# Up-projection of the latents in a two-block decoder kernel: query columns regrouped into rotary, turned and plain tiles, each emptied by one engine; values projected ahead of keys

## The reference, cut to what matters

```python
q = (_rmsnorm(q_lat, g_q_lat[i]) @ w_q_up[i]).reshape(bsz, s, N_HEADS, QK_DIM)      # 384 -> 8 x 96
kv = (_rmsnorm(kv_lat, g_kv_lat[i]) @ w_kv_up[i]).reshape(bsz, s, N_HEADS, NOPE_DIM + V_DIM)
q_nope, q_pe = q[..., :NOPE_DIM], q[..., NOPE_DIM:]                                 # 64 plain, 32 rotary
k_nope, v = kv[..., :NOPE_DIM], kv[..., NOPE_DIM:]
q_pe = _rope(q_pe, positions)        # [x1*cos - x2*sin, x2*cos + x1*sin]
k_pe = _rope(k_rope[:, :, None, :], positions)
```

## Time and profile before

| what | value |
|---|---|
| median of 3 runs | 2183.47 us (2182.7 to 2186.89) |
| the profiled execution's own time | 2190.65 us |
| its span in the profile | 2188.5 us |
| instructions | 30452 |
| mean granted clock of TensorE | 0.983 of full speed |
| busy: PE / DVE / ACT / POOL | 96% / 48% / 27% / 59% |

### The profile page before, as it was taken

One profiled execution on the slowest core, in us unless ns is written; L12 is line 12 of the kernel. 1 busy time (PEld: TensorE's weight loads), 2 busy tenths in 40 slices (PEclk: granted clock), 3 DMA queues, 4 the chain that ended last, 5 costly groups with the idle time before them and its releaser, 6 DMA issues. The chain is left out here.

```text
span 2188.5 us, 30452 instructions
## 1 busy us (share of the span) xinstructions
PE 2098.5 (96%) x10310; PEld 1689.6 (77%) x10310; DVE 1054.3 (48%) x1778; ACT 581.3 (27%) x1162; POOL 1283.6 (59%) x835
## 2 busy tenths in 40 slices
PE   7999899999999988999899999999999999999997
PEld 6877657788888867789788888888874467888886
DVE  4452555665552057556555555335337625555312
ACT  3112153322220044222332222000226714222100
POOL 6666445666667646432466666676665555666673
PEclk9999899999999989999999999999999999999998
DMA  5223263333333333211132323332420013323332
GB/s 174 92 89 100 66 81 115 102 97 97 96 96 115 106 108 97 68 59 40 40 96 96 96 96 96 106 105 87 145 87 1 1 58 96 96 96 96 96 106 77
DMA packets 55365, 195.25 MB, mean 89 GB/s; under 512 B 5971, under 2 KB 6163, under 8 KB 55028
## 3 DMA queue, kind: packets, MB, share of 16 engines
q1 hardware_dynamic: 50544, 181.95, 26.0%
q10 hardware_dynamic: 4740, 12.20, 2.7%
HBM read 188.10 MB, written 6.03 MB: 89 GB/s over the span
## 5 line engine op out<-in xcount | busy, mean ns | idle before, releaser
L708 POOL TENSOR_TENSOR wlo<-wraw,whi 128x1024 fp32r<-128x1024 f32 x339 | 828.9, 2445 | 28.3
L706 POOL TENSOR_SCALAR whi<-wraw 128x1024 fp32r<-128x1024 f32 x339 | 361.2, 1066 | 745.4 <-PE acc L779 665.1
L779 PE MATMUL acc<-xhi,whi 128*128 128x512 f32 x1784 | 704.1, 395 | 29.5 <-POOL wlo L708 11.5
L783 PE MATMUL acc<-xlo,whi 128*128 128x512 f32 x1784 | 699.2, 392 | 0.0
L782 PE MATMUL acc<-xhi,wlo 128*128 128x512 f32 x1784 | 699.2, 392 | 0.0
L779 PEld LDWEIGHTS acc<-xhi,whi 128*128 128x128 f32 x1784 | 337.8, 189 | 108.9 <-issue 24.7
L783 PEld LDWEIGHTS acc<-xlo,whi 128*128 128x128 f32 x1784 | 337.6, 189 | 71.3
L782 PEld LDWEIGHTS acc<-xhi,wlo 128*128 128x128 f32 x1784 | 338.0, 189 | 68.8
L782 PE MATMUL acc<-fhi,wlo 128*128 128x512 f32 x528 | 205.6, 389 | 0.0
L779 PE MATMUL acc<-fhi,whi 128*128 128x512 f32 x528 | 205.6, 389 | 0.0
L783 PE MATMUL acc<-flo,whi 128*128 128x512 f32 x528 | 205.5, 389 | 0.0
(11 more groups left out here) (379 smaller groups left out, 2488.2 us busy)
## 6 DMA issues: line engine op xcount, KB each, us to landing
wraw<-in_weights SPq DMA_DIRECT2D x339, 512.0 KB, 3.5
distances<-vr ACTq DMA_DIRECT2D x1, 3840.0 KB
toep<-distances ACTq DMA_DIRECT2D x4, 768.0 KB, 7.7
h<-in_x_t SPq DMA_DIRECT2D x4, 512.0 KB, 9.6
mem<-in_mem_t ACTq DMA_DIRECT2D x2, 1024.0 KB, 14.8
out_t<-h SPq DMA_DIRECT2D x8, 256.0 KB, 2.0
dmf<-in_sums ACTq DMA_DIRECT2D x1, 576.0 KB, 9.3
p_f<-in_p_t ACTq DMA_DIRECT2D x1, 512.0 KB, 3.4
```

The lines of the kernel that those rows point to most:

```text
L706: nc.gpsimd.tensor_scalar(whi[:, j, :], wraw[:, j % RAW, :], 1.0, 1.0, ALU.mult, ALU.mult).then_inc(sem["w_hi"], 1)
L708: nc.gpsimd.tensor_tensor(wlo[:, j, :], wraw[:, j % RAW, :], plain(whi[:, j, :]), ALU.subtract).then_inc(sem["w_split"], 1)
L779: m = nc.tensor.matmul(o, a_hi, b_hi, start=start, stop=False)
L783: m = nc.tensor.matmul(o, a_hi, b_lo, start=False, stop=stop)
```

## The change

On the host, the query weights are laid out anew: for each group of four heads (HR = 128 / 32) one tile of their rotary columns and one of their turned columns, and then four tiles with the plain columns of two heads each. The values' weights come ahead of the keys'.

On ACT, eight copies early in the kernel (behind the new semaphore `cs_ready`) spread cosine and sine to all 128 rows, in `cosr` and `sinr`. In the stage, DVE empties the four rotary and turned tiles: per group a 128-row product of the rotary tile into `tmp` (this gives it free), a 128-row product of the turned tile in its place in PSUM, and four additions of 32 rows each into `qf`, the last of which gives the turned tile free. ACT empties the four plain tiles, two copies each (`pair`), and two of the four key tiles; DVE empties the other two, both halves, and the value tiles. DVE counts the tiles that ACT empties as free once it sees `q_copied`.

On PE, the values are projected ahead of the keys, and `moving` opens each bank just before the first matmul into it, in all three of its calls.

```diff
-    q = np.concatenate([q, q[:, :, NOPE + h:], q[:, :, NOPE:NOPE + h]], 2).reshape(Q_LORA, HA * P)
+    turned = np.concatenate([q[:, :, NOPE + h:], q[:, :, NOPE:NOPE + h]], 2)
+    q = np.concatenate([x.reshape(Q_LORA, -1) for first in range(0, HA, HR) for x in (
+        q[:, first:first + HR, NOPE:], turned[:, first:first + HR])] + [q[:, :, :NOPE].reshape(Q_LORA, -1)], 1)
...
+    u.extend(_pack(_moving(kv[:, :, NOPE:].reshape(KV_LORA, -1), 0, HA * VD)))
     tiles(kv[:, :, :NOPE].reshape(KV_LORA, -1), range(0, HA * NOPE, P))
-    u.extend(_pack(_moving(kv[:, :, NOPE:].reshape(KV_LORA, -1), 0, HA * VD)))
...
         def moving(x_hi, x_lo, kts, n, tiles=TT, release=False):
-            for i in range(tiles):
-                open_tile(t + i)
...
                 for i in range(tiles):
+                    if k == 0:
+                        open_tile(t + i)
...
-        stationary(lathi[:, 3:5, :], latlo[:, 3:5, :], 2, 4, fresh=2)
+        pe.wait_ge(sem["x_ready"], xs + 2)
         xs += 2
         moving(lathi[:, 3:5, :], latlo[:, 3:5, :], 2, HA * VD)
+        mark["k"] = t
+        stationary(lathi[:, 3:5, :], latlo[:, 3:5, :], 2, 4)
...
         did(V.tensor_scalar(cs[r, :], cs[r, :], C("sign", p=r), None, ALU.mult))
+        n.tell(sem["cs_ready"])
...
-        for i in range(HA):
+        for first in range(0, HA, HR):
+            give(V.tensor_tensor(tmp[:, :], take(), cosr[:, :], ALU.mult))
             a = take()
-            n.did(V.tensor_tensor(qf[rot, i, :], a[rot, :], cs[rot, :], ALU.mult), sem["dve_step"], False)
+            did(V.tensor_tensor(a, a, sinr[:, :], ALU.mult))
+            for i in range(HR):
+                part = slice(i * ROPE, (i + 1) * ROPE)
+                ins = V.tensor_tensor(qf[rot, first + i, :], a[part, :], tmp[part, :], ALU.add)
+                if i < HR - 1:
+                    did(ins)
+                else:
+                    give(ins)
+        for i in range(HA // 2):
             dve.wait_ge(sem["q_copied"], i + 1)
-            ins = V.tensor_tensor(tmp[rot, :], a[swapped, :], cs[swapped, :], ALU.mult)
-            give(ins)
-            did(V.tensor_tensor(qf[rot, i, :], qf[rot, i, :], tmp[rot, :], ALU.add))
-        for i in range(4):
+            n.tell(sem["acc_free"])
+        t_add(HA // 2)
+        for i in range(TT):
+            give(V.tensor_copy(va[:, i, :], take()))
+        for i in range(0, 4, 2):
             a = take()
             n.did(V.tensor_scalar(kf[0:NOPE, 2 * i, :], a[0:NOPE, :], -QK ** -0.5, None, ALU.mult), sem["dve_step"], False)
-            dve.wait_ge(sem["q_copied"], HA + i + 1)
-            give(V.tensor_scalar(kf[0:NOPE, 2 * i + 1, 0:P], a[NOPE:P, 0:P], -QK ** -0.5, None, ALU.mult))
-        for i in range(TT):
-            give(V.tensor_copy(va[:, i, :], take()))
+            give(V.tensor_scalar(kf[0:NOPE, 2 * i + 1, :], a[NOPE:P, :], -QK ** -0.5, None, ALU.mult))
+            dve.wait_ge(sem["q_copied"], HA // 2 + i // 2 + 1)
+            n.tell(sem["acc_free"])
+            t_add(1)
...
+        act.wait_ge(sem["cs_ready"], 1)
+        for i in range(HR):
+            part = slice(i * ROPE, (i + 1) * ROPE)
+            n.did(A.activation(cosr[part, :], cs[NOPE:QK, :], ACT.Copy), sem["act_step"], False)
+            n.did(A.activation(sinr[part, :], cs[QK:P, :], ACT.Copy), sem["act_step"], False)
...
-        for i in range(HA):
-            tile = mark["q"] + i
+        def pair(to, tile, first, scale):
             act.wait_ge(sem["acc_ready"], tile + 1)
-            n.did(A.activation(qf[0:NOPE, i, :], acc[0:NOPE, tile % 4, :], ACT.Copy), sem["q_copied"], False)
-        for i in range(4):
-            tile = mark["q"] + HA + i
-            act.wait_ge(sem["acc_ready"], tile + 1)
-            n.did(A.activation(kf[0:NOPE, 2 * i + 1, P:], acc[NOPE:P, tile % 4, P:], ACT.Copy, scale=-QK ** -0.5),
-                  sem["q_copied"], False)
-        act.wait_ge(sem["q_copied"], HA + 4)
+            for e in range(2):
+                n.did(A.activation(to[0:NOPE, first + e, :], acc[e * NOPE:(e + 1) * NOPE, tile % 4, :], ACT.Copy, scale=scale),
+                      sem["q_copied" if e else "act_step"], False)
+        for i in range(HA // 2):
+            pair(qf, mark["q"] + HA // 2 + i, 2 * i, 1.0)
+        for i in range(1, 4, 2):
+            pair(kf, mark["k"] + i, 2 * i, -QK ** -0.5)
+        act.wait_ge(sem["q_copied"], HA // 2 + 2)
```

More of the change, by code:

```diff
@@ L29 @@
 QK = NOPE + ROPE
+HR = P // ROPE
 ROPE_THETA = 10000.0
@@ L409, in build_program @@
     spare = fix("spare", [P, 1])
+    cosr, sinr = (nc.alloc_sbuf_tensor_at(name, [P, S], F32, offset=mkt_at + at) for name, at in (("cosr", 4096), ("sinr", 6144)))
     decay = fix("decay", [P, GH * TT])
@@ L528, in build_program @@
              "in_chunk in_p ple_sig gl_raw gl_ln in_masks f_ready gates_raw o_raw oroot_ready "
-             "gates_ready hid_raw act_step in_row in_mem0 in_mem1 z_done hi_ready kpe_ready q_copied e_copied fm_ready fh_ready "
+             "gates_ready hid_raw act_step in_row in_mem0 in_mem1 z_done hi_ready kpe_ready cs_ready q_copied e_copied fm_ready fh_ready "
              "dm_ready la_raw lah_ready ml_ready me_ready mn_ready mt_ready mc_ready gn_ready o_ready").split()
```

## The result

In the comparison that followed, ten runs of each kernel, the changed one took 2171.24 us in the median (2168.88 to 2179.36), the one before 2186.53 us (2182.7 to 2188.72). The ratio is 0.9934, with an interval of 0.9922 to 0.9946: 14.4 us faster, 11.8 to 17.1. A second comparison, six runs of the changed kernel, gave a median of 2171.07 us and 0.9923 (0.9909 to 0.9937): 16.8 us faster, 13.8 to 19.9. Two runs of the kernel before in that second comparison, at 2378.04 and 4475.45 us, stand apart from all others and are left out of the ratios. The forecast was faster by 19.0 us. Direction and place were right; the size is outside the first interval and near the end of the second.

A forecast was written before the change was run, and what follows sets the result against it. The prediction took PE, busy 96% of the span and waiting for banks DVE frees late, as the bound. 16.7 us in the stage and 2.3 later made 19.0 us off the median: 2164.5 us, range 2161.5 to 2171.5.

The forecast's parts named there:

- The bound and the cause: In the stage, PE waits 9.6 us for banks DVE hands back late, behind ACT's key copies and three instructions a head.
- The layout of the new stage: Latents to a projection: 27.2 us without PE waits; ACT pairs some 1.1 us, smallest margin 0.7 us.
- The choice by operands: New DVE additions, one input in PSUM and one in SBUF, priced at 0.70 us, not 1.146 as L1793.
- The size of the stage's loss: Stage takes 43.90 us instead of 27.2: 16.7 us lost, 9.6 in waits and 7.1 in late or slow matmuls.
- The later calls of `moving`: Last layer's two value streams: opening banks one by one gains 2.3 us, bounds nothing and 2.6; both waits under 0.3.
- The sum: Whole kernel: 16.7 us in the stage and 2.3 later make 19.0 us, the whole tail moving up.
- The first: Rival, chance 0.15: POOL's subtractions block the stage's additions, PE waits for turned tiles, 5.1 us lost: 2169.6 us.
- The second: Rival, chance 0.04: time is given back at attention, or DVE's other work fills the stage; say 2181 us.
- the third: Rival, chance 0.03: PE without pauses from gates to attention gets a lower clock, making the kernel slower, 2195 us.
- The range: Whole kernel: 2161.5 to 2171.5 us, from the forecast's bounds with scatter to the first rival with its scatter.

The follow-up runs named there:

- values_at_once: The changed kernel, but the stage's own value call opens all four banks before its first matmul; median 2172.72 us, ratio 0.9943 to the kernel before.
- sums_in_sbuf: The changed kernel, but the turned tile's product goes to SBUF, so the additions have both inputs there; median 2176.93 us, ratio 0.9957 to the kernel before.
- first_early: The changed kernel, but the first of the two later value streams opens all four banks first, the second one by one; median 2172.93 us, ratio 0.9936.
- before_look2: The kernel before, unchanged, traced again for its stage alone; the stage took 41.45 us at a clock of 0.88.

## Why the prediction was right and where it was wrong

- **The bound and the cause.** Right. PE was held by banks that DVE gave back late, DVE by ACT's key copies and three instructions a head. With the cause removed the stage takes 27.20 us, the 27.2 that 120 matmuls were said to take.
- **The layout of the new stage.** Right, with one duration too short: no wait of PE, the additions at 0.689 us (0.70 taken), the first group's end at 215.39 (4.3 us behind DVE's start, as laid out). A pair on ACT takes 1.21 us and not 1.1, which left 0.6 us at the fourth value bank. values_at_once waited 1.6 us where 1.4 were named.
- **The choice by operands** instead of by place: right, and shown from both sides, by the change's own additions during POOL's subtractions and by sums_in_sbuf. The rule of the Trainium skill that is named with it ("SBUF — State Buffer", "Who interferes with whom") agrees with both: eight additions of 0.69 us with one input in SBUF, 5.55 and 5.76 us for four with two. It agrees with the window additions too (6.11 us instead of 4.40), whose collision is the one I didn't look for.
- **The size of the stage's loss: the first step that failed.** "16.7 us are lost: 9.6 us in the waits, and 7.1 us in matmuls that come late or slowly after them" was read off one execution and set against the median. In five executions the loss was 14.3 to 16.7, in the mean 15.7. The 7.1 us are not a property of the kernel: how much of the time behind a pause passes at the lower clock changes from one execution to the next (0.84 and 0.88 for the same stage). This term was 1.0 us too large. That the profiled execution stood 7.2 us above the median of three was noted, and then nothing was taken off for it.
- **The later calls of `moving`: the second step that failed, and the larger one.** "1.22 - 0.1 and 1.42 - 0.2, a gain of 2.3 us" is 0.5 us up to the first query copy, 1.8 too many, and it is not made in the way that was named. Both waits were to fall under 0.3 us; the first went, the second rose from 1.3 to 1.6 us, and the second stream came 1.0 us later than before. I followed banks and copies, but not the queue that the earlier start releases: POOL's split, which waits for PE's first matmul of a unit and which I counted among what simply moves up. It moved ahead of DVE's window additions, which read two inputs from SBUF, and these lost 1.7 us; the subtraction behind them lost another 1.1. first_early, which takes the early start away and has the old additions again, shows that this is the cause. What is left of gain at the first query copy came from the clock behind the third wait, which no term of the sum held.
- **The sum.** With what the traces show, 42.9 - 27.2 = 15.7 and 0.5 make 16.2 us: inside the intervals of both comparisons (11.8 to 17.1 and 13.8 to 19.9 us); with 1.2 for the later calls, the mean to the program's end, 16.9. Nothing else is needed for the missing gain; whether something below 2 us is hidden in the rest can't be told from these runs.
- **The rivals.** The first (which the working calls the second rival in two places) happened in neither trace of the changed kernel. Its price of 5.1 us is 5.0 by its own terms (2.9 us of waits and 7.1 / 9.6 of that), and it was 33.85 - 27.20 = 6.65 us when brought about. The second, time given back at attention or behind it, didn't happen either: from the first matmul of the a projection to the last key copy the two traces of the changed kernel took 1276.5 and 1278.4 us, the five of the kernel before 1276.4 to 1280.3. Nor did the third (a lower clock for a denser PE): the mean clock rose, from 0.984 to 0.988 in the medians of the timed runs.
- **The range** was argued from a time before of 2183.47 us, the median of three; ten runs had 2186.53. The 3.1 us between the two are nearly half of the 6.7 us by which the median of 2171.24 missed the 2164.5. The range's upper end, 2171.5, leaves 12.0 us of gain against the former and 15.0 against the latter, while the measured gain is 14.4: the median of 2171.24 lies just inside it, the time before less 14.4 us, 2172.1, just outside. It should have been wider for that alone. Its ends were not made alike either: 2169.6 with the 2.5 us of scatter that the lower end has would have been 2172.1, and the lower end 2161.7.

## What to carry to other kernels

A pause of PE costs its own length and a share of slow matmuls that differs between executions, so size it from several traces, or state the gain as an interval with "waits alone" as one end (here 9.6) and one trace's whole loss as the other.

Let a release of PE be followed into every queue that it sets going: a weight split that started 1.3 us earlier on POOL blocked two DVE instructions with two SBUF inputs, and the microsecond won was gone two steps later. Keep one operand of DVE's short instructions in PSUM where POOL is busy: it was worth 6.65 us here, for two changed lines. Opening banks one at a time is as short an edit, but look at each call: it took 4.1 us off the stage of the kernel before, and in the last layer it made the second stream 1.0 us later until the first call was opened early again.

## What the runs showed of the hardware that I had not expected

- POOL's copy of 1.05 us blocks DVE's additions with two SBUF inputs as its subtraction of 2.4 us does, and what such an addition of 0.69 us loses is what POOL's instruction still has to run when it begins, less 0.14 to 0.16 us. That held in all twenty blocked additions of the stage, for rests from 0.64 to 2.23 us: 0.5 to 0.7 us lost in before_look2, 1.8 to 1.9 in the first trace, 0.6 to 0.9 behind a copy and 2.1 behind a subtraction in sums_in_sbuf.
- Blocking goes both ways. POOL's copy of 1.05 us took 1.96 us when it began 0.8 us behind the window additions (1532.40), and the additions 6.11 us instead of 4.40 when POOL began first.
- The clock behind the same pauses differs between executions of one kernel: 0.84 or 0.88 over the stage. The two traced executions at 0.84 took 2190.65 and 2190.27 us, the three at 0.88 from 2185.69 to 2187.65.
